# Quartered expert-weight loads inside narrow slots of a top-4-of-32 MoE kernel

## The reference, cut to what matters

```python
logits = hf @ w_r + b_r
top_val, top_idx = lax.top_k(logits, TOP_K)          # 4 of 32
...
def expert_block(args):
    xb, e = args
    u = xb @ w_in[e] + b_in[e]                        # 1024 -> 2048
    return _clamped_swiglu(u) @ w_out[e] + b_out[e]   # 1024 -> 1024
```

## Time and profile before

| | |
|---|---|
| median of 3 runs | 1867.73 us (1866.98 to 1868.55) |
| profiled execution, its own time | 1869.45 us |
| its span | 1868.0 us |
| TensorE clock granted, mean | 0.996 |
| TensorE matmul busy | 1820.3 us, 97% |
| weight loads of TensorE busy | 1661.3 us, 89% |
| VectorE, ScalarE, GpSimd busy | 59%, 25%, 12% |

### The profile page before, as it was taken

One profiled execution on the slowest core, in us unless ns is written; L12 is line 12 of the kernel. 1 busy time (PEld: TensorE's weight loads), 2 busy tenths in 40 slices (PEclk: granted clock), 3 DMA queues, 4 the chain that ended last, 5 costly groups with the idle time before them and its releaser, 6 DMA issues.

```text
span 1868.0 us, 51572 instructions
## 1 busy us (share of the span) xinstructions
PE 1820.3 (97%) x22829; PEld 1661.3 (89%) x22829; DVE 1107.4 (59%) x2818; ACT 463.6 (25%) x1358; POOL 218.6 (12%) x250
## 2 busy tenths in 40 slices
PE   7999999998999999999999999999999999999997
PEld 4665865567999999999999999999999999999996
DVE  2754776775655555656565655556574756555465
ACT  2204654431212121212121212121221212122213
POOL 2003000000101010101010101101020101011012
PEclk9999999999999999999999999999999999999998
DMA  8981111126979797969797997979897999999996
GB/s 322 356 182 47 49 75 51 46 79 255 348 269 358 269 366 286 363 252 368 258 364 287 366 341 275 387 270 380 285 389 267 377 341 359 340 353 336 349 340 216
DMA packets 150229, 523.98 MB, mean 281 GB/s; under 512 B 10042, under 2 KB 15826, under 8 KB 150002
## 3 DMA queue, kind: packets, MB, share of 16 engines
q1 hardware_dynamic: 131202, 467.68, 68.4%
q0 software_dynamic: 17200, 52.59, 8.4%
q10 hardware_dynamic: 1600, 0.36, 0.1%
HBM read 485.34 MB, written 34.21 MB: 278 GB/s over the span
## 4 chain that ended last, share of the span: by engine, by line
PE 94%; DMA 2%; DVE 2%; issue 1%; ACT 1%; POOL 0%; SPq 0%; POOLq 0%; DVEq 0%; ACTq 0%
PE ps L1820 49%; PE ps L1842 24%; PE ps L1682 6%; PE ps L1603 4%; PE ps L1690 3%; PE ps L1581 1%; PE ps L1536 1%; PE ps L1553 1%; PE ps L1632 1%; PE ps L1624 1%; PE ps L1599 1%; PE ps L1662 1%; PE ps L1503 1%; DMA xr<-acc_d 1%; PE ps L1716 0%
## 5 line engine op out<-in xcount | busy, mean ns | idle before, releaser
L1820 PE MATMUL ps<-xr,ring 128*64 128x128 f32 (+6 forms) x4864 | 502.3, 289 | 0.7 <-issue 0.7
L1820 PEld LDWEIGHTS ps<-xr,ring 128*128 128x128 f32 (+1 forms) x4864 | 498.5, 168 | 2.6 <-issue 1.3
L1842 PE MATMUL ps<-U,ring 128*64 128x120 f32 (+11 forms) x6656 | 470.0, 270 | 2.8 <-ACT U L911 2.4
L1842 PEld LDWEIGHTS ps<-U,ring 128*64 128x64 f32 (+1 forms) x6656 | 464.2, 149 | 4.7 <-issue 4.1
L1820 PE MATMUL ps<-U,ring 128*64 128x120 f32 (+4 forms) x8448 | 432.0, 259 | 10.0 <-issue 9.8
L1820 PEld LDWEIGHTS ps<-U,ring 128*64 128x64 f32 (+1 forms) x8448 | 425.9, 139 | 15.1 <-issue 14.2
L1387 DVE TENSOR_SCALAR U<-ps,U 128x120 f32<-128x120 f32 (+11 forms) x256 | 90.9, 355 | 468.1 <-PE ps L1820 466.0
L1324 DVE STREAM_TRANSPOSE xr<-U 32x256 f32<-32x256 f32 (+1 forms) x484 | 227.9, 471 | 91.6 <-DMA U<-xn_d,U 84.7
L897 ACT ACTIVATE U<-U 128x120 f32<-128x120 f32 (+11 forms) x256 | 80.1, 313 | 811.6 <-DVE U L1387 800.4
L1336 DVE STREAM_TRANSPOSE xr<-U 32x256 f32<-32x256 f32 (+1 forms) x484 | 230.0, 475 | 9.3
L911 ACT ACTIVATE U<-ps,U,modT 128x120 f32<-128x120 f32 (+11 forms) x256 | 112.4, 461 | 263.8 <-PE ps L1842 253.6
(11 more groups left out here) (248 smaller groups left out, 1194.7 us busy)
## 6 DMA issues: line engine op xcount, KB each, us to landing
ring<-in_moe_w SPq DMA_DIRECT2D x191, 2048.0 KB, 13.3
U<-in_w_mod SPq DMA_DIRECT2D x8, 2048.0 KB, 11.9
ring<-in_w_mod SPq DMA_DIRECT2D x3, 2048.0 KB, 18.9
acc_d<-xr SPq DMA_DIRECT2D x10, 512.0 KB, 3.5
xr<-in_x SPq DMA_DIRECT2D x8, 512.0 KB, 9.4
ring<-in_w_qkv SPq DMA_DIRECT2D x2, 2048.0 KB, 11.0
ring<-in_w_o SPq DMA_DIRECT2D x2, 2048.0 KB, 8.3
xn_d<-U SPq DMA_DIRECT2D x8, 512.0 KB, 2.6
```

Of the source, the lines that this page charges most:

```text
L1820: last = pe.matmul(bank(j % 4)[lo:hi, s * 256:s * 256 + n], w[:, k, s, (j % 2) * P + lo:(j % 2) * P + hi], columns_of(r)[:, k, 0:n], start ...
L1842: last = pe.matmul(bank(4 + m % 4)[lo:hi, 0:n], w[:, k, (m % 4) * P + lo:(m % 4) * P + hi], actT[:, k, 0:n], start=(k == 0), stop=(k == KT ...
```

## The change

A piece that is asked for while a narrow slot between wide ones runs is loaded in its four runs of 0.5 MB, each a DMA of its own; all other pieces stay whole. Runs 0 and 2 count on `s_wl[p]`, runs 1 and 3 on a new semaphore `s_wodd`. Run 0 waits until run 2 (or the whole) of the piece before has landed, run 1 until run 3 of the quartered piece before has, run 2 for run 0, run 3 for run 1. TensorE waits for both semaphores. To free a semaphore, `s_cs` of the start of the program is folded into `s_ca`.

```diff
+LAST_MIXED = max(r for r in range(E) if WIDTHS[r] > P)
...
+        def asked_in_narrow(r, p):
+
+            if r == 0 or r > LAST_MIXED + 1:
+                return False
+            return p == NPIECE - 1 if not wide(r) else load_step(r, p) < 16
+
+        def load_step(r, p):
+
+            if wide(r):
+                return (steps_light if WIDTHS[r - 1] <= LIGHT else steps_spread)[p]
+            return (steps_full if r > 2 and WIDTHS[r - 2] <= LIGHT and wide(r - 1) else steps_to)[p]
+
+        def transfers_of(r, p):
+
+            return 2 if (r, p) == (0, 0) or asked_in_narrow(r, p) else 1
+
         def loads_of(r, p):
-            return (r + 2) * 16 if p == 0 else (r + 1) * 16
+            return 16 * sum(transfers_of(q, p) for q in range(r + 1))
+
+        def odd_quarters(r, p):
+
+            return 16 * 2 * sum(asked_in_narrow(q // NPIECE, q % NPIECE) for q in range(r * NPIECE + p + 1))
...
-                        if wide(r):
-                            steps = steps_light if WIDTHS[r - 1] <= LIGHT else steps_spread
-                        else:
-                            steps = steps_full if r > 2 and WIDTHS[r - 2] <= LIGHT and wide(r - 1) else steps_to
-                        sp.wait_ge(s_mm, (r - 1) * 16 + steps[p])
+                        sp.wait_ge(s_mm, (r - 1) * 16 + load_step(r, p))
...
+                    elif asked_in_narrow(r, p):
+                        before_it = (r, p - 1) if p else (r - 1, NPIECE - 1)
+                        sp.wait_ge(s_wl[before_it[1]], loads_of(*before_it))
+                        load_runs(sp, e, p, 0, 1, s_wl[p])
+                        if odd_quarters(r, p) > 32:
+                            sp.wait_ge(s_wodd, odd_quarters(r, p) - 32)
+                        load_runs(sp, e, p, 1, 2, s_wodd)
+                        sp.wait_ge(s_wl[p], loads_of(r - 1, p) + 16)
+                        load_runs(sp, e, p, 2, 3, s_wl[p])
+                        sp.wait_ge(s_wodd, odd_quarters(r, p) - 16)
+                        load_runs(sp, e, p, 3, 4, s_wodd)
                     else:
                         load_piece(sp, e, p, s_wl[p])
...
                         pe.wait_ge(s_wl[j // 2], loads_of(r, j // 2))
+                        if asked_in_narrow(r, j // 2):
+                            pe.wait_ge(s_wodd, odd_quarters(r, j // 2))
...
                 pe.wait_ge(s_wl[5], loads_of(r, 5))
+                if asked_in_narrow(r, 5):
+                    pe.wait_ge(s_wodd, odd_quarters(r, 5))
```

More of the change, by code:

```diff
@@ L274, in program @@
         s_v = sem("dve_chain"); s_a = sem("act_chain")
-        s_pl = sem("place_row_ready"); s_cs = sem("sigmoid_c"); s_ca = sem("silu_c")
+        s_pl = sem("place_row_ready"); s_ca = sem("sigmoid_c_then_silu_c"); s_wodd = sem("odd_piece_quarter_loaded")
         s_first = sem("vecs_transposed_then_bias_row_product"); s_vecT = sem("vecT_ready")
@@ L740, in _ @@
             act.wait_ge(s_c, 16)
-            act.activation(cS[:, :], cT[:, :], ACT.Sigmoid).then_inc(s_cs, 1)
+            act.activation(cS[:, :], cT[:, :], ACT.Sigmoid).then_inc(s_ca, 1)
             act.wait_ge(s_first, 1)
@@ L958, in link @@
                 dve.wait_ge(s_v, vc[0])
-            dve.wait_ge(s_cs, 1)
+            dve.wait_ge(s_ca, 1)
             dve.tensor_tensor(out=cA[:, :], in0=cT[:, :], in1=cS[:, :], op=ALU.mult).then_inc(s_ca, 1)
-            dve.wait_ge(s_ca, 1)
+            dve.wait_ge(s_ca, 2)
             dve.wait_ge(s_const, 1)
@@ L1512, in mod_partials @@
                 else:
-                    pe.wait_ge(s_ca, 2)
+                    pe.wait_ge(s_ca, 3)
                 w = stages[stage_of[n]].rearrange("p (t n) -> p t n", t=KT)
```

## The result

The changed kernel takes **1883.78 us** (median of 6 runs, 1881.01 to 1887.0) against 1868.19 us for the kernel before (6 runs), a ratio of 1.0085 with a 95% interval of 1.0072 to 1.0098: 16 us slower. 1855.7 us were forecast, with a range up to 1864.0.

What follows compares the result with a forecast made beforehand. TensorE bounds the kernel, with 14.4 us of narrow-slot stalls from late instruction packets; less 2 us that stay and 0.4 us of turns, 12.0 us off 1867.73 gives 1855.7 us, range 1852.5 to 1864.0.

Steps and rivals of the forecast that it cites:

- What bounds the kernel, and what the stalls are: TensorE bounds it; 14.4 us idle in narrow slots' up steps are instruction packets late behind queued weight pieces.
- What stays: Narrow slots: 2 us of instruction stalls remain, bounds 0 and 6.6, plus about 0.4 us of slots' turns.
- the 1.0 us of turns in its lower bound: Turns from slot to slot, subtracted in the gain's lower bound: 14.4 - 6.6 - 1.0 = 6.8 us.
- Are the pieces late now?: Quartered pieces in narrow and following wide slots: all land in time, with 10 us and more to spare.
- The time of a piece: A quartered piece takes two rounds of two quarters, about 4.8 us each, so 9.6 us.
- The start of the stream: In an 88 slot piece 5 is asked at the slot's start and lands at about 10 us.
- the right sign: Slower: SP's waits for landings throttle the stream of pieces, about 1905 us at 10 us a round; chance 0.07.
- A round over 7.9 us: Point where the slower rival sets in: a round of two quarters over 7.9 us in 88 slots, 8.7 in 104.
- the place named: Where the slower rival has TensorE wait: piece 0 at a wide slot's first step, behind the narrow slot's piece 5.
- Part of it: Rival: engine holds some 16 packets of a queue, so gain is only 4.8 to 7.2 us, 1860.5 to 1863; chance 0.22.
- no change: Rival: the instruction packet's wait is not set by queue length, the 14.4 us stay, 1867.7 us; chance 0.11.
- the rule that it named with the latter: DMA engines alternate queues after each packet; read as a 0.16 us wait per instruction packet, no gain, contradicted by the trace.

Runs made afterwards that it cites:

- unsplit_88: The kernel before with its three 88 slots computed by full 128x128 weight loads, not two halves, no DMA changed: 1898.79 us, ratio 1.0160.
- spread_three: Against the changed kernel, only pieces 5, 0 and 1 are quartered in narrow slots 1 to 23, pieces 2 and 3 stay whole: 1855.82 us, ratio 0.9934.
- no_head_wait: The changed kernel without the wait of a quartered piece's first quarter for the landing of the piece before it: 1866.74 us, ratio 0.9986.
- relieved: The changed kernel with four whole pieces per pair, slots 14 to 23, loading a quarter of their bytes (stale weights): 1851.04 us against 1862.37 for the kernel before.
- all_at_once: The changed kernel with the four quarters issued one behind the other, without waits between them or for the piece before: 1869.4 us, ratio 1.0008.
- spread_two: Against the changed kernel, only pieces 5 and 0 are quartered in slots 13 to 23, pieces 1, 2 and 3 stay whole: 1856.13 us, ratio 0.9940.

## Why the prediction was wrong

*What bounds the kernel, and what the stalls are: right.* Four runs bear on it. They go with fewer bytes queued (the change, 14.4 to 2.7 us idle), come back when the quarters are all queued (12.4 us), are in between with one whole piece (5.9 us), and go with half the instructions and no DMA changed (unsplit_88). Why an instruction packet has to wait behind what is queued is not shown.

*What stays: right.* I took 2 us of stalls and 0.4 us of slots' turns; the narrow up steps are idle 2.7 us with everything in. The 12.0 us of gain were there: 10.8 us by the end of slot 15, and 12.4 us in spread_three (1868.23 to 1855.82), whose time is the forecast's. Two small things in the working change nothing: a block of an 88 slot lasts 4.90 us in the earlier trace rows where the prediction reckons with 4.86, and the 1.0 us of turns in its lower bound is given without a source.

*"Are the pieces late now?": this is the step that failed.* It answered no, "all hidden under TensorE's own work, with 10 us and more to spare", and so put the waits for pieces at nothing. They took 20.5 us of TensorE's time (10.7 + 6.9 + 2.9, slots 16 to 23), and the lower clock after four of them some 6.6 us more (last section). Three things went into it.

The time of a piece was sized right. I put it at 9.6 us; in slots 13 and 14 of the changed kernel 17 quarters were issued between 1045.9 and 1080.3, which is 34.4 / 4 = 8.6 us a piece; the last three of these pieces, from 1052.8 on, took 27.5 / 3 = 9.2. In slots 15 and 16 the 20 quarters went out between 1138.0 and 1183.0, 45.0 / 19 x 4 = 9.5 us a piece.

The start of the stream was wrong. I wrote that "piece 5 is asked at its start and lands at about 10". The first quarter waits for the landing of whole piece 4, and that was not at the slot's start: the first quarter of slot 13 went out at 1045.9, 9.3 us into it, that of slot 15 at 1138.0, 14.6 us into it, and that of slot 17 at 1232.9, 21.3 us into it. Piece 4 itself stood behind other whole pieces: the prediction took the 10.2 us of one piece in slot 3, while the median of the 191 whole pieces of the kernel before was 13.3 us from issue to landing. In the meantime SP issued nothing. SP's timeline around slot 15, which begins at 1123.3:

```profile
1116.54 0.37 SPq L407 DMA_DIRECT2D ring<-in_moe_w  x1
1137.95 10.92 SPq L411 DMA_DIRECT2D ring<-in_moe_w  x6
```

In the kernel before, piece 5 was issued at 1134.7, 0.3 us into slot 15, whatever piece 4 did. no_head_wait undoes this and gets about 17 of the 28 us of the change's distance to spread_three back (1883.8 to 1866.7). Piece 3 of wide slots was to land 11 us into them; its last quarter was only issued 22.7 us into slot 16 and 26 us into slot 18, where it is needed after some 25 us.

And I judged each slot afresh. I had the spill of 11 us into the wide slot, checked that each piece there still came in time, and stopped. The wide slots had no DMA time left (share 1.00), and I had not looked at them. The account belongs to the pair: 87.8 us with 0.89 busy leaves 9.6 us; a quartered piece takes 8.6 to 9.5 us where a whole one at full load takes 5.0 (512 packets at the 389 in 3.8 us of the earlier trace rows), about 4 us more. By this estimate two or three of them cost 8 to 12 us, five cost 20. What is missing is carried into the next pair, so that the first waits come in slot 16 and grow. The dose shows it: TensorE waited for pieces 0 us with two and with three of them, 9.0 us with four and 20.5 us with five, and 0 again with five where the pairs were given DMA time (relieved). The slots 16 to 22 together lasted 307.4 us with three, 320.9 with four and 337.1 with five, where they took 310.3 in the kernel before, some 3 us of it the stalls of slots 17, 19 and 21 (1.25, 0.66 and 1.05 us, stretch less busy weight loads).

*The rivals.* I gave 0.07 to the right sign, with a point that was wrong and a place that was partly right. "A round over 7.9 us" was never reached: rounds took 4.3 to 4.8 us (half of 8.6 to 9.5), and the pieces were late all the same. At the first step of a wide slot, the place named, TensorE waited 6.9 us of the 20.5, in slots 18, 20 and 22; the rest stood at pieces 5, 2 and 3. "Part of it" and "no change" are out, since the stalls fell from 14.4 to 2.7 us.

The prediction misread the rule that it named with the latter. "DMA: Bandwidth & Descriptors" of the Trainium skill, section "Queues, rings and completion order", has an engine take turns by packets, but a packet there is typically 9 to 17 descriptors; the prediction took one 4 KB packet of the profile for it. If each of those is one descriptor, a turn is an estimated 1.4 to 2.7 us (9 to 17 times 0.156 us) and not 0.16, and the 1.8 us by which the packet of slot 3 started later than the unloaded one (3.3 less 1.5) lies within it. So the trace does not contradict that rule as the prediction says, and the rule does not forecast "no change"; no run here shows whether it is the cause. How many packets an engine holds of a queue was not measured.

*What I took for harmless, rightly:* the 44 waits of TensorE (slots 1 to 13 show none), the 132 more DMAs (all_at_once), the later slots 24 to 31, whose weight loads show no new idle time.

The best version is spread_three, 12.4 us under the kernel before and 28 us under the change; spread_two is 0.3 us from it, less than can be told.

## What to carry to other kernels

A throttle on loads is paid for in queue time, and the account is to be made over the whole period of the schedule, not per load: take the DMA share of the full period before, multiply the idle rest out, and compare it with the extra time of all throttled transfers. Whoever lets a load wait for the landing of the one before it makes its start depend on that one's queue: look up when that lands. Quarter only about as many as the idle time pays for; here three of five gave all of the gain, at an estimated 12 us a pair against 9.6 us idle, and the time by which pieces came early seems to have covered the rest.

## What was unexpected about the hardware

A wait for a piece can cost more than itself. After the wait before slot 18, 2.64 us of idle matmuls, the granted clock was 0.53 over 3.5 us, nearly all of it at the lower of the two levels, and then 1.00 again; the stretches 1252.3 to 1255.8 and 1256 to 1260 of the changed kernel:

```profile
1252.30:1255.80 3.50, 3.50 (x15) 3.50 (x16) 0.00 (x0) 0.00 (x0) 0.00 (x0) 0.53 0.75 259
1256.00:1260.00 4.00, 4.00 (x33) 4.00 (x33) 1.59 (x7) 0.33 (x1) 0.00 (x0) 1.00 0.86 268
```

15 matmuls ran in 3.5 us where 29 would at the second row's pace: 1.7 us lost. This followed four of the 13 waits in slots 16 to 22: the two longest of slot 18 and one each of slots 20 and 22. After the others, one of 2.13 us among them, the clock stayed at 1.00. By the granted clocks of slots 18, 20 and 22 (0.94 of 56.2 us, 0.97 of 53.0 and 52.7) the lower level cost 3.4 + 1.6 + 1.6 = 6.6 us, a quarter of the 26.8 us that slots 16 to 22 got longer. "DMA: Bandwidth & Descriptors" of the Trainium skill, section "Bandwidth", advises transfers of 1 MiB or more for 75% of the peak, from loads that GpSimd issued. Here, in SP's queue, transfers of 0.5 MB one behind the other were as good as 2 MB ones (all_at_once, 1869.4 us and no late piece); what cost was to wait for landings between them.

And the products of an 88 slot took 29.3 us by twice as many half weight loads, 42.8 us by full ones.
